# Weights of v in pairs, h in rows of 512 tokens, gates and gelus in DRAM by fours, gates stored from the sync engine

## The chip, the core and the metric

One core of a Trainium2 chip runs one transformer block (batch 1, 512 tokens, width 1024) from one launch. The metric is the device time of that launch in microseconds. TensorE's clock is granted by the chip at 1.2 or 2.4 GHz; a granted clock of 1.00 in the profile is 2.4 GHz.

## The reference

The block is adaLN, a mixer of three kinds of attention, and a feed-forward layer of the PEER kind. The change touches the last. For each token it scores 8 heads x 2 x 128 keys, takes the best 16 of 16384 experts for each head, and adds up their rows:

```
q = einsum(h, wq);  s = einsum(q, sub_keys)          # 2 x 128 keys per head
top, eidx = the 16 best of the 16384 pairs;  g = softmax(top)
a = gelu(einsum(u[eidx], h));  out = einsum(g * a, v[eidx])
x = x + g2 * out;  return rmsnorm(x, final_g)
```

All is float32. u and v have 16384 rows of 1024 numbers, 64 MB each.

## The kernel before

The 512 tokens are four tiles of 128. For the first tile (128 tokens x 128 chosen experts) GpSimd gathers one row of u and one of v per token and expert (L1203 to L1219), and VectorE does the product with h and the sum into y0 (L2121, L2098). For the other three tiles, 384 tokens, nothing is gathered: the 16384 experts are taken in 128 chunks of 128, and every expert is computed for every token. Three things are made for each chunk:

- a = u h: TensorE, 24 matmuls of 384 columns (`a_chunk`, L843 to L860). Each float32 operand is split into a high part in the fast format (float32r) and a low part, the rest, and three products are taken: u_hi h_hi, u_hi h_lo, u_lo h_hi. ScalarE copies u_raw to u_hi (`u_high`, L1428), VectorE or GpSimd makes u_lo = u_raw - u_hi (L2131, L2002; L1200 for the first 17 chunks), and ScalarE takes gelu of a into one of 8 slots of a_act (L1471).
- the gates: a matrix of 128 experts x 384 tokens that holds the softmax weight where a token has chosen an expert and 0 elsewhere. They are made before the loop, in 12 blocks of 32 tokens x all 16384 experts, and put in DRAM.
- v: TensorE, 18 matmuls of 512 columns (`v_chunk`, L897 to L909) that add w_hi v_hi, w_hi v_lo, w_lo v_hi to six banks of PSUM, where w is gate times gelu.

h_hi and h_lo are laid out [tile, k, 128 tokens] (L162), so the 384 tokens of one k are three pieces of 128 columns, 4 KB apart. `q_passes` (L804) reads the same two tensors for wq.

**Order of the work.** It is written out by hand for every engine, with semaphores. TensorE does the first u chunks while VectorE chooses the experts. Then come three parts, one for each tile (the gates' stage): in a part four blocks of gates (`tb`), each of eight groups. A group is small matmuls of hot rows into bank T (L885), made by VectorE (L2057, L2059) and copied by ScalarE into g_out (L1505, two buffers of 16 KB a partition, `g_out[tb % 2]`), and a quarter of a chunk of u beside them. Between the parts only chunks of u run (`BETWEEN`, L366: chunks 0 to 23, 32 to 35, 44 to 51, 60 to 63), while VectorE decodes the next tile's experts; the last of them is cut in two halves, around three transposes into bank G (L870).

At the end of a block ScalarE waits for its last copy and issues the store of 2 MB (L1511, L1512). The chunks' gelus of 0 to 55 are stored too (`spill`, L1483) and come back for the late stage (L1096).

```
gates = nc.dram_tensor("gates", [DT // GB, P, NCHUNK, GB], f32).ap()     # L296
spill = nc.dram_tensor("spill", [SPILL, P, DT], f32).ap()                # L297
BETWEEN = [range(0, 24), range(32, 36), range(44, 52), range(60, 64)]    # L366
return BETWEEN[tb // 4].stop + 2 * (tb % 4)                              # beside(tb), L376
```

So a block's run in DRAM is 16 KB a partition (128 experts' numbers x 32 tokens), and one load for four chunks (`load_g`, L1088) takes 12 runs of 512 B a partition.

**The sync engine's queue** (L1076 to L1132) issues the loads of u (each waits until the chunk two before it is split, s_ulo), of v (four buffers, waits for s_vlo), of gates and of the gelus. `load_g(0)` comes after the loads of u for chunks 64 and 65, and waits for all stores of gates (s_gst).

**The loop** over the chunks of v (`chunk_loop`, L314) has 128 turns. In turns 0 to 62 TensorE does a chunk of v and one of u (up to 1291 us of the profile), afterwards (the late stage) one of v alone. VectorE's `weigh` (L2069 to L2089) does for every chunk: the product w_f (L2076), its high part w_hi (L2085), its low part w_lo (L2087), 384 columns each; then v_lo (L2108), the first tile's products and sums, and u_lo (L2131). ScalarE's `parts` (L1524) does v_hi, the small gelus and weights of the first tile, u_hi and the gelu. The last four chunks have buffers of their own (`..._end`, L198 to L201).

Of the kernel before, what the change touches and what calls it, by code (L numbers as in the profile page):

```python
# [6 lines left out]
P = 128  # L7
D, S = 1024, 512
KD = D // P
# [9 lines left out]
GT = 1  # L19
# [78 lines left out]
def peer_block_kernel(nc, x, c_col, norm1_col, w_ada, b_ada, w_in, w_out, lam_vecs, subln_row, sinks_row,  # L98
# [4 lines left out]
    with ctx:  # L103
# [9 lines left out]
        def at(name, kib, shape, dt=f32):  # L113
# [34 lines left out]
        wo_hi = [at(f"wo_hi{k}", kib, [P, D], f32r) for k, kib in enumerate((24, 28, 44, 76))]  # L148
# [13 lines left out]
        h_hi = at("h_hi", 32, [P, NT, KD, P], f32r)  # L162
        h_lo = at("h_lo", 64, [P, NT, KD, P], f32r)
# [14 lines left out]
        y0 = at("y0", 32, [P, D])  # L178
        g_in = at("g_in", 56, [P, 2, DT // GB, 4, GB])
# [5 lines left out]
        u_lo = [at(f"u_lo{j}", kib, [P, D], f32r) for j, kib in enumerate((92, 84))]  # L185
# [5 lines left out]
        w_f = at("w_f", 128, [P, DT])  # L191
        w_hi = at("w_hi", 130, [P, 2, DT], f32r)
        w_lo = at("w_lo", 133, [P, 2, DT], f32r)
        rows = [at(f"row{j}", k, [P, D]) for j, k in enumerate((104, 108, 136, 168, 176, 184,
                                                                     140, 144, 148, 152, 156, 160))]
        junk = at("junk", 180, [P, D])
# [4 lines left out]
        w_lo_end = at("w_lo_end", 176, [P, TAIL, DT], f32r)  # L201
# [94 lines left out]
        gates = nc.dram_tensor("gates", [DT // GB, P, NCHUNK, GB], f32).ap()  # L296
        spill = nc.dram_tensor("spill", [SPILL, P, DT], f32).ap()  # L297
# [6 lines left out]
        def after(eng, s, n):  # L304

            if isinstance(n, int) and n < 1:
                return
            eng.wait_ge(s, n)

# [109 lines left out]
        def out_hi(k, half=None):  # L419

            if k == 4:
                return v_r[:, :, 192:448] if half is None else v_r[:, 2 * half:2 * half + 2, 192:448]
            t = wo_hi[k] if k < 4 else wo_hi_c[k - 5]
            return t[:, :] if half is None else t[:, half * 512:half * 512 + 512]

# [30 lines left out]
        def _(pe):  # L456
# [347 lines left out]
            def q_passes(e, tiles):  # L804

                ps = bank[f"S{e % 3}"][:, tiles.start * P:tiles.stop * P]
                pe.wait_ge(s_qhi, e + 1)
                pe.wait_ge(s_qlo, e + 1)
                for k in range(KD):
                    kk = slice(k * P, k * P + P)  # L810
                    pe.matmul(ps, wq_hi_of(e)[:, kk], h_hi[:, tiles, k, :], start=(k == 0), stop=False)
                    pe.matmul(ps, wq_hi_of(e)[:, kk], h_lo[:, tiles, k, :], start=False, stop=False)
                    mm = pe.matmul(ps, wq_lo[e % 2][:, kk], h_hi[:, tiles, k, :], start=False, stop=(k == KD - 1))
# [29 lines left out]
            def a_chunk(i, c, part=range(KD)):  # L843
# [10 lines left out]
                for k in part:  # L854
                    kk = slice(k * P, k * P + P)
                    pe.matmul(ps[:, 0:DT], u_hi[q][:, kk], h_hi[:, GT:NT, k, :], start=(k == 0), stop=False)  # L856
                    pe.matmul(ps[:, 0:DT], u_hi[q][:, kk], h_lo[:, GT:NT, k, :], start=False, stop=False)  # L857
                    mm = pe.matmul(ps[:, 0:DT], u_lo[q][:, kk], h_hi[:, GT:NT, k, :], start=False, stop=(k == KD - 1))  # L858
# [38 lines left out]
            def v_chunk(i, c):  # L897

                pe.wait_ge(s_w, i + 1)
                pe.wait_ge(s_vlo, i + 1)  # L900
                q = c % 2
                first = isinstance(i, int) and i == 0
                for t in range(NT - GT):
                    tt = slice(t * P, t * P + P)
                    for n, (w, v) in enumerate(((w_hi, v_hi), (w_hi, v_lo), (w_lo, v_hi))):
                        for half in range(2):
                            mm = pe.matmul(y_bank[t][half][:, :], w[:, q, tt], v[:, q, half * 512:half * 512 + 512],  # L907
# [3 lines left out]
            def last_v_chunks():  # L911
# [8 lines left out]
                def chunk_ready(m):  # L920
                    pe.wait_ge(s_w, m + 1)
# [68 lines left out]
        def _(sp):  # L990
# [1242 lines left out]
```

## Time and profile before

| | |
|---|---|
| three runs | 1567.2, 1567.73, 1568.44 us; median 1567.73 |
| the profiled execution: span from first to last instruction | 1565.4 us |
| its own whole time | not given by the profile |
| TensorE matmul / weight load | 1527.4 us (98%) / 1363.9 us (87%) |
| VectorE / ScalarE / GpSimd | 1337.7 us (85%) / 660.1 us (42%) / 487.5 us (31%) |
| mean granted clock of TensorE | 0.995 |
| DMA | 398.77 MB, mean 255 GB/s |
| store of a block of gates, issue to landing, median of 12 | 6.8 us |

"Busy" counts matmuls as they overlap, so it says that TensorE had work, not that it ran at its best. Register, branch and semaphore instructions are not counted. A row of the timeline has the start, the duration, engine, line, operation, and output<-inputs; in square brackets stands the idle time before it and what ended it. bank_S, bank_T, bank_O and bank_G are banks of PSUM; PEld is TensorE's weight load. The rows stand in a section further down.

### The profile page before, as it was taken

How to read it: one execution, taken by the hardware profiler on the slowest of the kernel's cores; microseconds unless marked ns; L12 is line 12 of the kernel's file. 1: busy time of each engine (PE TensorE's matmuls, PEld its weight loads, DVE VectorE, ACT ScalarE, POOL GpSimd, SP SyncE). 2: the span in 40 equal slices, each digit the busy share in tenths (PEclk: the TensorE clock that was granted, in tenths of full speed). 3: DMA queues.
4: the chain of work that ended last, by engine and by line, in shares of the span. 5: the costliest groups of instructions: out<-in, count | busy, mean ns of one | idle time of the engine just before them, and what ended most of it. 6: DMA issues, size and time to landing. Idle time of an engine off the chain costs nothing.

```text
span 1565.4 us, 24588 instructions
## 1 busy us (share of the span) xinstructions
PE 1527.4 (98%) x8275; PEld 1363.9 (87%) x8275; DVE 1337.7 (85%) x2877; ACT 660.1 (42%) x1143; POOL 487.5 (31%) x450
## 2 busy tenths in 40 slices
PE   4999999999999999999999999999999999999997
PEld 4887767888999999999999999999999998888886
DVE  5788666549999989899698898899999998999977
ACT  3444554233344757657433333343333332333232
POOL 1121300033450000020355455456566663233000
PEclk9999999999999999999999999999999999999999
DMA  9754410132355565676899999999999999999772
GB/s 366 270 174 148 148 68 0 55 95 82 118 169 180 194 230 199 229 248 251 298 393 330 350 340 343 346 337 371 372 378 372 368 345 355 376 350 352 241 244 104
DMA packets 160467, 398.77 MB, mean 255 GB/s; under 512 B 11753, under 2 KB 75369, under 8 KB 158705
## 3 DMA queue, kind: packets, MB, share of 16 engines
q1 hardware_dynamic: 112992, 227.06, 41.7%
q0 software_dynamic: 36864, 134.23, 23.2%
q10 hardware_dynamic: 10514, 36.30, 5.9%
q8 instruction: 47, 0.77, 0.2%
q14 instruction: 50, 0.41, 0.1%
HBM read 359.27 MB, written 38.27 MB: 254 GB/s over the span
## 4 chain that ended last, share of the span: by engine, by line
PE 83%; DVE 13%; DMA 1%; ACT 1%; issue 1%; ACTq 0%; DVEq 0%; SPq 0%
PE bank_S L907 16%; PE bank_T L907 11%; PE bank_O L858 6%; PE bank_O L856 6%; PE bank_O L857 6%; PE bank_T L885 5%; PE bank_G L907 5%; PE bank_S L856 3%; PE bank_S L857 3%; PE bank_S L858 3%; PE bank_O L643 2%; PE bank_S L610 2%; DVE mod_acc L1909 1%; DVE v_sb L1902 1%; DVE v_sb L1915 1%; DVE si L1921 1%
## 5 line engine op out<-in xcount | busy, mean ns | idle before, releaser
L1462 ACT ACTIVATE v_hi<-v_raw 128x1024 fp32r<-128x1024 f32 x124 | 131.7, 1062 | 333.9 <-PE bank_G L907 330.9
L1434 ACT ACTIVATE u_hi<-u_raw 128x1024 fp32r<-128x1024 f32 x128 | 135.9, 1061 | 243.0 <-PE bank_O L858 122.8
L1213 POOL COPY stage<-eidx 128x1 uint32<-128x1 uint32 (+1 forms) x128 | 75.7, 591 | 461.8 <-DVE eidx L2030 207.7
L1217 POOL DMA_INDIRECT row<-in_peer_u,stage x128 | 148.1, 1157 | 103.8 <-POOL stage L1213 103.8
L856 PE MATMUL bank_S<-h_hi,u_hi 128*128 128x384 f32 x512 | 179.7, 351 | 0.5 <-DVE u_lo L2002 0.5
L858 PE MATMUL bank_O<-h_hi,u_lo 128*128 128x384 f32 x512 | 171.9, 336 | 0.0
L856 PE MATMUL bank_O<-h_hi,u_hi 128*128 128x384 f32 x512 | 171.7, 335 | 0.0
L858 PE MATMUL bank_S<-h_hi,u_lo 128*128 128x384 f32 x512 | 171.5, 335 | 0.0
L857 PE MATMUL bank_O<-h_lo,u_hi 128*128 128x384 f32 x512 | 171.5, 335 | 0.0
L857 PE MATMUL bank_S<-h_lo,u_hi 128*128 128x384 f32 x512 | 171.4, 335 | 0.0
L2098 DVE SCALAR_TENSOR_TENSOR y<-row,wgt,y 128x1024 f32<-128x1024 f32 x128 | 165.9, 1296 | 0.0
L2108 DVE TENSOR_TENSOR v_lo<-v_raw,v_hi 128x1024 fp32r<-128x1024 f32 x124 | 152.0, 1226 | 12.1 <-ACT v_hi L1462 0.6
L2121 DVE SCALAR_TENSOR_TENSOR junk<-row,h 128x1024 f32<-128x1024 f32 x128 | 155.8, 1217 | 0.0
L1217 POOL DMA_INDIRECT row<-in_peer_v,stage x128 | 141.6, 1106 | 41.9 <-issue 30.3
L907 PE MATMUL bank_S<-v_hi,w_lo 128*128 128x512 f32 x372 | 125.4, 391 | 0.0
L907 PE MATMUL bank_S<-v_lo,w_hi 128*128 128x512 f32 x372 | 125.3, 391 | 0.0
L907 PE MATMUL bank_S<-v_hi,w_hi 128*128 128x512 f32 x372 | 125.2, 391 | 0.0
L1505 ACT ACTIVATE g_out<-bank_T 128x512 f32<-128x512 f32 x96 | 104.7, 1122 | 46.6 <-PE bank_T L885 38.2
L2057 DVE TENSOR_SCALAR hot_i<-iota_k,cols 128x128 f32<-128x128 f32 x384 | 106.6, 341 | 1.0 <-PE bank_T L885 0.2
L885 PE MATMUL bank_T<-hot_i,hot_j 128*128 128x128 f32 x768 | 101.8, 275 | 1.2 <-DVE hot_j L2059 1.2
L885 PEld LDWEIGHTS bank_T<-hot_i,hot_j 128*128 128x128 f32 x768 | 97.6, 191 | 3.6 <-issue 2.1
L856 PEld LDWEIGHTS bank_O<-h_hi,u_hi 128*128 128x128 f32 x512 | 96.1, 188 | 2.5
(370 smaller groups left out, 3647.8 us busy)
## 6 DMA issues: line engine op xcount, KB each, us to landing
u_raw<-in_u_t SPq DMA_DIRECT2D x128, 512.0 KB
v_raw<-in_peer_v SPq DMA_DIRECT2D x128, 512.0 KB
gates<-g_out ACTq DMA_DIRECT2D x12, 2048.0 KB, 6.8
g_in<-gates SPq DMA_DIRECT2D x32, 768.0 KB
ada_late<-in_w_ada SPq DMA_DIRECT2D x8, 2048.0 KB, 8.4
spill<-a_act ACTq DMA_DIRECT2D x56, 192.0 KB, 2.1
a_act<-spill SPq DMA_DIRECT2D x14, 768.0 KB, 10.6
w_raw<-in_w_in SPq DMA_DIRECT2D x20, 512.0 KB, 4.1
```

The source lines that it names most:

```text
L856: pe.matmul(ps[:, 0:DT], u_hi[q][:, kk], h_hi[:, GT:NT, k, :], start=(k == 0), stop=False)
L857: pe.matmul(ps[:, 0:DT], u_hi[q][:, kk], h_lo[:, GT:NT, k, :], start=False, stop=False)
L858: mm = pe.matmul(ps[:, 0:DT], u_lo[q][:, kk], h_hi[:, GT:NT, k, :], start=False, stop=(k == KD - 1))
L885: mm = pe.matmul(ps[:, tok * P:tok * P + P], hot_j[:, b % 2, tok, :], hot_i[:, b % 2, tok, :], start=True, stop=True)
L907: mm = pe.matmul(y_bank[t][half][:, :], w[:, q, tt], v[:, q, half * 512:half * 512 + 512], start=(first and n == 0), stop=False)
L1217: pool.indirect_dma_start(rows[slot][:, :], None, table[:, :], bass.IndirectOffsetOnAxis(stage[:, place:place + 1], 0))\
L1434: act.activation(u_hi[c % 2][:, :], u_raw[:, c % 2, :], ACT.Copy).then_inc(s_uhi, 1)
L1462: act.activation(v_hi_end[:, i % TAIL, :] if end else v_hi[:, c % 2, :], v_raw[c % 4][:, :], ACT.Copy)\
L2057: dve.tensor_scalar(hot_i[:, B % 2, tok, :], iota_k[:, :], cols[:, 0, n:n + 1], cols[:, 2, n:n + 1], ALU.is_equal, ALU.mult)
L2098: dve.scalar_tensor_tensor(out=y0[:, :], in0=rows[2 * place + 1][:, :], scalar=wgt[:, q], in1=y0[:, :], op0=ALU.mult, op1=ALU.add).then_in ...
L2108: dve.tensor_tensor(lo[:, q, :], v_raw[c % 4][:, :], hi[:, q, :].bitcast(f32), ALU.subtract)\
L2121: dve.scalar_tensor_tensor(out=junk[:, :], in0=rows[2 * place][:, :], scalar=1.0, in1=h2[:, 0, :], op0=ALU.mult, op1=ALU.mult, accum_out=d ...
```

## The change

- h_hi and h_lo are [k, 512 tokens], so the moving operand of `a_chunk` and `q_passes` is one run. The two tensors' first 128 columns of each k (the first tile's) are no longer needed after wq: u_lo of every second chunk lies in h_lo's, y0 in h_hi's, each in eight pieces of 128 (`by_k`). GpSimd's `split_u(1)` waits until the last q is done.
- The product is made for two chunks at once, in place in g_in, by VectorE; ScalarE copies its high part (`w_high`), VectorE subtracts (`w_low`). w_hi and w_lo have two buffers of two chunks. The product of a pair is made one chunk ahead, w_high is issued at the end of ScalarE's even chunks.
- gates is [partition, four of chunks, block, 4, 32], spill [four, partition, 4, 384]. A block's store now writes 32 runs of 512 B a partition, a load of gates reads one run of 6 KB a partition, and so does a load of gelus.
- The stores of gates go from ScalarE's to the sync engine's queue, after the load of u four chunks past `beside(tb)`.
- The product of the first tile (L2121) writes over the gathered row instead of into junk; rows, g_in, w_hi, w_lo and w_lo_end have other places in SBUF. The first tile's last squares go to rows[2].

```diff
-        h_hi = at("h_hi", 32, [P, NT, KD, P], f32r)
-        h_lo = at("h_lo", 64, [P, NT, KD, P], f32r)
+        h_hi = at("h_hi", 32, [P, KD, S], f32r)
+        h_lo = at("h_lo", 64, [P, KD, S], f32r)
-        y0 = at("y0", 32, [P, D])
-        g_in = at("g_in", 56, [P, 2, DT // GB, 4, GB])
+        y0 = at("y0", 32, [P, KD, S])[:, :, 0:P]
+        g_in = [at(f"g_in{j}", kib, [P, DT // GB, 4, GB]) for j, kib in enumerate((56, 182))]
-        u_lo = [at(f"u_lo{j}", kib, [P, D], f32r) for j, kib in enumerate((92, 84))]
+        u_lo = [at("u_lo0", 92, [P, KD, P], f32r)[:, :, :], h_lo[:, :, 0:P]]
-        gates = nc.dram_tensor("gates", [DT // GB, P, NCHUNK, GB], f32).ap()
-        spill = nc.dram_tensor("spill", [SPILL, P, DT], f32).ap()
+        gates = nc.dram_tensor("gates", [P, NCHUNK // 4, DT // GB, 4, GB], f32).ap()
+        spill = nc.dram_tensor("spill", [SPILL // 4, P, 4, DT], f32).ap()
...
-                    pe.matmul(ps[:, 0:DT], u_hi[q][:, kk], h_hi[:, GT:NT, k, :], start=(k == 0), stop=False)
+                    pe.matmul(ps[:, 0:DT], u_hi[q][:, kk], h_hi[:, k, GT * P:S], start=(k == 0), stop=False)
...
-                pe.wait_ge(s_w, i + 1)
+                pe.wait_ge(s_w, over(i, c, 2) + 1)
...
-                    after(sp, s_pw, 4 * (q - 1))
-                    sp.dma_start(g_in[:, parity, :, :, :].rearrange("p b i t -> p b (i t)"),
-                                 gates[:, :, bass.ds(chunk_of(4 * q, late), 4), :].rearrange("b p i t -> p b (i t)"))\
+                    after(sp, s_w, 2 * (q - 1))
+                    own = q - MAIN // 4 if late or (isinstance(q, int) and 4 * q >= MAIN) else q + SPILL // 4
+                    sp.dma_start(g_in[parity][:, :, :, :].rearrange("p b i t -> p (b i t)"),
+                                 gates[:, bass.ds(own, 1), :, :, :].rearrange("p o b i t -> p (o b i t)"))\
...
+            def store_gates(tb):
+
+                sp.wait_ge(s_gt, (tb + 1) * (GB // 4))
+                sp.dma_start(gates[:, :, tb, :, :].rearrange("p q i t -> p q (i t)"),
+                             g_out[tb % 2][:, :, :].rearrange("p (q i) t -> p q (i t)", i=4)).then_inc(s_gst[tb % 2], 16)
+
+            STORES = {beside(tb) + 4: tb for tb in range(BLOCKS)}
             for i in range(2, EARLY):
                 load_u(i, i)
+                if i in STORES:
+                    store_gates(STORES[i])
                 m = i - (EARLY - 5)
...
+                if i == 1:
+                    taken(pool, ("q", 2 * PH - 1))
                 pool.wait_ge(s_uhi, i + 1)
...
+            def w_high(i, c):
+
+                if not within(i):
+                    return
+                if at_end(i):
+                    act.wait_ge(s_acc, PH * TOPK)
+                else:
+                    after(act, s_yv, i - 2)
+                act.wait_ge(s_pw, over(i, c, 2) + 1)
+                act.activation(weight_pair(w_hi, w_hi_end, i, c), gate_pair(c), ACT.Copy).then_inc(s_whi, 1)
...
-                    act.wait_ge(s_gt, (tb + 1) * (GB // 4))
-                    act.dma_start(gates[tb].rearrange("p i t -> p (i t)"),
-                                  g_out[tb % 2][:, :, :].rearrange("p i t -> p (i t)")).then_inc(s_gst[tb % 2], 16)
...
+                if c % 2 == 0:
+                    w_high(m + 2, c + 2)
...
+                dve.tensor_tensor(gate_pair(c), by_block(a_act[:, slot:slot + 2, :]), gate_pair(c), ALU.mult)\
+                   .then_inc(s_pw, 1)
+
+            def w_low(i, c):
+
+                dve.wait_ge(s_whi, over(i, c, 2) + 1)
+                if not at_end(i):
+                    after(dve, s_yv, i - 2)
+                dve.tensor_tensor(weight_pair(w_lo, w_lo_end, i, c), gate_pair(c),
+                                  weight_pair(w_hi, w_hi_end, i, c).bitcast(f32), ALU.subtract).then_inc(s_w, 1)
...
             def chunk(i, c, late, numbers):
-                weigh(i, c, late)
+                if c % 2 == 0:
+                    w_low(i, c)
+                else:
+                    product(i + 1, c + 1)
```

## Rows read from the trace of the kernel before

**Rows 1.** Table of stretches: length, busy us and instructions of each engine, TensorE's clock, DMA share, GB/s.

```profile
500.00:600.00 100.00, 99.15 (x677) 97.53 (x676) 93.72 (x231) 62.80 (x70) 0.00 (x0) 1.00 0.56 200
...
768.00:1031.00 263.00, 263.00 (x1330) 239.22 (x1329) 236.65 (x310) 99.06 (x194) 141.60 (x148) 1.00 0.95 349
```

**Rows 2.** Timeline of TensorE, early stage: start us, us, engine, line, operation.

```profile
429.01 0.33 PE L856 MATMUL bank_S<-h_hi,u_hi 128*128 128x384 f32 x1
...
432.13 0.33 PE L856 MATMUL bank_S<-h_hi,u_hi 128*128 128x384 f32 x1
```

**Rows 3.** Chain of waits, loop and late stage: start us, us, what.

```profile
1100.32 1.62 PE bank_S L907 x7
1108.63 1.62 PE bank_S L907 x7
...
1454.62 1.59 PE bank_S L907 x7
1458.70 1.59 PE bank_S L907 x7
```

**Rows 4.** Timeline of TensorE after a group of small matmuls, gates' stage.

```profile
589.40 0.42 PE L856 MATMUL bank_S<-h_hi,u_hi 128*128 128x384 f32 x1
589.66 0.34 PE L857 MATMUL bank_S<-h_lo,u_hi 128*128 128x384 f32 x1
```

**Rows 5.** Groups by line and shape, whole span: count | busy us, mean ns | idle us before.

```profile
L2108 DVE TENSOR_TENSOR v_lo<-v_raw,v_hi 128x1024 fp32r<-128x1024 f32 x124 | 152.0, 1226 | 12.1 <-ACT v_hi L1462 0.6 <-DVE w_lo L2087 0.3
...
L1434 ACT ACTIVATE u_hi<-u_raw 128x1024 fp32r<-128x1024 f32 x128 | 135.9, 1061 | 243.0 <-PE bank_O L858 122.8 <-PE bank_S L858 79.3 <-DMA u_raw<-in_u_t 18.2
...
L2076 DVE TENSOR_TENSOR w_f<-a_act,g_in 128x384 f32<-128x384 f32 x128 | 70.4, 550 | 1.1 <-ACT a_act L1471 1.0
...
L2087 DVE TENSOR_TENSOR w_lo<-w_f,w_hi 128x384 fp32r<-128x384 f32 x124 | 69.4, 559 | 4.3
...
L2085 DVE CAST w_hi<-w_f 128x384 fp32r<-128x384 f32 x124 | 45.2, 365 | 47.5 <-PE bank_G L907 40.4 <-DVE w_f L2076 0.4
...
L1200 POOL TENSOR_TENSOR u_lo<-u_raw,u_hi 128x1024 fp32r<-128x1024 f32 x17 | 40.8, 2398 | 35.7 <-ACT u_hi L1434 35.7
...
L1471 ACT ACTIVATE a_act<-bank_O 128x384 f32<-128x384 f32 x64 | 30.3, 474 | 4.7 <-PE bank_O L858 4.7
```

**Rows 6.** DMA, 762 to 764 us (load of gates), then 652 to 656 us (store).

```profile
DMA packets 1224, 0.63 MB, mean 315 GB/s; under 512 B 8, under 2 KB 1222, under 8 KB 1224
...
DMA packets 108, 1.77 MB, mean 442 GB/s; under 512 B 0, under 2 KB 0, under 8 KB 0
```

**Rows 7.** Timeline of ScalarE, VectorE and TensorE at the end of the first part.

```profile
580.69 1.06 ACT L1434 ACTIVATE u_hi<-u_raw 128x1024 fp32r<-128x1024 f32 x1 [3.92 <-DMA u_raw<-in_u_t]
...
581.86 1.23 DVE L2002 TENSOR_TENSOR u_lo<-u_raw,u_hi 128x1024 fp32r<-128x1024 f32 x1 [1.75 <-ACT u_hi L1434]
...
588.52 1.13 PE L885 MATMUL bank_T<-hot_i,hot_j 128*128 128x128 f32 x8 [0.40 <-DVE hot_j L2059]
```

**Rows 8.** Timeline of VectorE and TensorE at the end of the second part.

```profile
661.49 1.22 DVE L2002 TENSOR_TENSOR u_lo<-u_raw,u_hi 128x1024 fp32r<-128x1024 f32 x1 [1.60 <-ACT u_hi L1434]
...
663.23 0.33 PE L856 MATMUL bank_S<-h_hi,u_hi 128*128 128x384 f32 x1
```

**Rows 9.** Timeline at the end of the third part and the start of the loop.

```profile
745.63 0.43 SPq L1085 DMA_DIRECT2D v_raw<-in_peer_v  x1
...
747.41 0.34 ACTq L1512 DMA_DIRECT2D gates<-g_out  x1
...
757.72 1.23 DVE L2002 TENSOR_TENSOR u_lo<-u_raw,u_hi 128x1024 fp32r<-128x1024 f32 x1 [3.95 <-ACT u_hi L1434]
...
759.58 0.33 PE L856 MATMUL bank_S<-h_hi,u_hi 128*128 128x384 f32 x1
...
765.45 0.57 DVE L2076 TENSOR_TENSOR w_f<-a_act,g_in 128x384 f32<-128x384 f32 x1 [1.02 <-ACT a_act L1471]
...
767.89 0.63 PE L907 MATMUL bank_S<-v_hi,w_hi 128*128 128x512 f32 x2
```

More of the change, by code:

```diff
@@ L308, in after, with half_columns, by_k, gate_pair @@
             eng.wait_ge(s, n)
+        def half_columns(h, i, half):
+            return h[:, 4 * half:4 * half + 4, i * P:i * P + P]
+        def by_k(row):
+            return row.rearrange("p (k c) -> p k c", k=KD)
+        def gate_pair(c):
+            return g_in[c // 4 % 2][:, :, c % 4:c % 4 + 2, :].rearrange("p b i t -> p i b t")
+        def by_block(pair):
+            return pair.rearrange("p i (b t) -> p i b t", t=GB)
+        def weight_pair(w, w_end, i, c):
+            if at_end(i):
+                q = i % TAIL
+                return by_block(w_end[:, q:q + 2, :])
+            return by_block(w[c // 2 % 2][:, :, :])
         def within(i, last=NCHUNK - 1):
@@ L422, in out_hi, with in_pieces @@
                 return v_r[:, :, 192:448] if half is None else v_r[:, 2 * half:2 * half + 2, 192:448]
+            if k in (2, 3):
+                last = (h_hi, h_lo)[k - 2][:, :, (NT - 1) * P:S]
+                return last if half is None else last[:, 4 * half:4 * half + 4, :]
             t = wo_hi[k] if k < 4 else wo_hi_c[k - 5]
             return t[:, :] if half is None else t[:, half * 512:half * 512 + 512]
+        def in_pieces(k, whole):
+            pieces = {2: KD, 3: KD, 4: NT}
+            return whole.rearrange("p (t c) -> p t c", t=pieces[k]) if k in pieces else whole
         def wq_hi_of(e):
@@ L804, in q_passes @@
             def q_passes(e, tiles):
+                columns = slice(tiles.start * P, tiles.stop * P)
                 ps = bank[f"S{e % 3}"][:, tiles.start * P:tiles.stop * P]
@@ L855, in a_chunk @@
                     kk = slice(k * P, k * P + P)
-                    pe.matmul(ps[:, 0:DT], u_hi[q][:, kk], h_hi[:, GT:NT, k, :], start=(k == 0), stop=False)
-                    pe.matmul(ps[:, 0:DT], u_hi[q][:, kk], h_lo[:, GT:NT, k, :], start=False, stop=False)
-                    mm = pe.matmul(ps[:, 0:DT], u_lo[q][:, kk], h_hi[:, GT:NT, k, :], start=False, stop=(k == KD - 1))
+                    pe.matmul(ps[:, 0:DT], u_hi[q][:, kk], h_hi[:, k, GT * P:S], start=(k == 0), stop=False)
+                    pe.matmul(ps[:, 0:DT], u_hi[q][:, kk], h_lo[:, k, GT * P:S], start=False, stop=False)
+                    mm = pe.matmul(ps[:, 0:DT], u_lo[q][:, k, :], h_hi[:, k, GT * P:S], start=False, stop=(k == KD - 1))
                 if part[-1] == KD - 1:
@@ L1798, in h_low @@
                 dve.wait_ge(s_hhi, 2 * i + half + 1)
-                part = slice(4 * half, 4 * half + 4)
-                dve.tensor_tensor(h_lo[:, i, part, :], ps[:, :].rearrange("p (a b) -> p a b", b=P),
-                                  h_hi[:, i, part, :].bitcast(f32), ALU.subtract)\
+                dve.tensor_tensor(half_columns(h_lo, i, half), ps[:, :].rearrange("p (a b) -> p a b", b=P),
+                                  half_columns(h_hi, i, half).bitcast(f32), ALU.subtract)\
                    .then_inc(freeing(("h2T", i, half)), 1)
@@ L2097, in row_sum @@
                 dve.wait_ge(s_got[2 * place + 1], 16 * (over(n, c, RING) + 1))
-                dve.scalar_tensor_tensor(out=y0[:, :], in0=rows[2 * place + 1][:, :], scalar=wgt[:, q], in1=y0[:, :],
+                dve.scalar_tensor_tensor(out=y0, in0=by_k(rows[2 * place + 1][:, :]), scalar=wgt[:, q], in1=y0,
                                          op0=ALU.mult, op1=ALU.add).then_inc(s_acc, 1)
@@ L2120, in chunk @@
                     dve.wait_ge(s_got[2 * place], 16 * (over(n, g, RING) + 1))
[L2121 removed]
+                    dve.scalar_tensor_tensor(out=rows[2 * place][:, :], in0=rows[2 * place][:, :], scalar=1.0,
+                                             in1=h2[:, 0, :],
                                              op0=ALU.mult, op1=ALU.mult, accum_out=dots[:, g % 4:g % 4 + 1])\
```

86 lines of the change are left out of this document (37 added, 49 removed).

## The prediction

> **What bounds the kernel now.** I read the table of stretches first. In 500 to 600 us TensorE's matmuls are busy 99.15 of 100 us, in 768 to 1031 all 263 of 263, at a granted clock of 1.00 (2.4 GHz); VectorE stands at 93.72 and 236.65 in the same stretches [rows 1]. So from the gates' stage to the end of the loop over the chunks of v the time is the number of TensorE's instructions times its step, and what another engine saves is worth nothing unless TensorE waits for it. Next the step itself. A busy share of 100% could hide slow matmuls, so I took starts from the chain and the timeline. In the early stage 18 matmuls of 384 columns take 432.13 - 429.01 = 3.12 us, 173.3 ns each [rows 2]; in the late stage a chunk of v (18 matmuls of 512 columns) takes 1458.70 - 1454.62 = 4.08 us, 226.7 ns each [rows 3]. At 2.4 GHz both are the columns plus 32 cycles. The first has the moving operand h_hi in three pieces of 128 columns, the second a plain row: same surcharge. In the loop a chunk of v with one of u takes 1108.63 - 1100.32 = 8.31 us [rows 3] against 4.08 + 24 x 0.1733 = 8.24.
>
> TensorE has few waits after that. Where it nearly waits is what decides here: at the ends of the three parts of the gates' stage, where a chunk of u must be loaded while a block of gates is being stored.
>
> **h in rows of 512 tokens.** It removes the pieces of the moving operand: 24 matmuls in each of 128 chunks read 384 columns in one run. As the pieces cost nothing in the steps above, I cost this at nothing. The bound on the gain is what the steps leave over: 63 chunks x 0.07 us = 4.4 us in the loop, and in the gates' stage the step after the small matmuls, 589.66 - 589.40 = 0.26 us instead of 0.173, 96 times: 8.3 us [rows 4]. The low part of every second chunk of u and y0 now lie in eight pieces inside h_lo and h_hi. VectorE pays nothing for pieces: its product with the gates reads twelve pieces of 32 in 550 ns, its plain subtraction of the same size takes 559 [rows 5]. GpSimd's subtraction is known plain alone, 2398 ns [rows 5]. A chunk of u must be split while TensorE does one, 24 x 0.1733 = 4.16 us: 1.06 on ScalarE, 2.40 on GpSimd, some 0.3 of hops, which leaves 0.4.
>
> **Weights in pairs.** For two chunks VectorE now pays 2 x (550 + 365 + 559) = 2948 ns [rows 5]. Afterwards it does two instructions of 768 columns. Between 384 columns (559) and 1024 (v_lo, 1226) a column costs 1.04 ns [rows 5], so 768 take 0.95 us each, 1.90 in all: 0.52 us less per chunk. ScalarE gets one of 768: between 474 (384 columns) and 1061 (1024) 0.83 us per pair [rows 5]. None of this is on the path: TensorE does not wait for VectorE in the loop [rows 1]. ScalarE's new instruction waits for the product that VectorE makes at the start of the next chunk; behind it on ScalarE stands v_hi of the same later chunk. Even so 0.83 + 1.06 us are over before VectorE, busy at least 0.95 + 1.22 + 1.22 us in that chunk, asks for v_hi. Gelu's slots are free earlier than before. Taken at 0.
>
> **Gates and gelus by fours.** A block of gates is 2 MB. It was written in runs of 16 KB, and is now written in runs of 512 B; the loads in the loop change the other way, from 512 B to 6 KB. The number of short runs is the same (12 blocks x 4096 against 32 loads x 1536, 49152 each), but they move from the loop, where nobody waits for DMA, to the gates' stage. What short runs cost I take from loads, since the trace has no such store: 1224 packets, 1222 of them under 2 KB, in 2 us, so 612 a microsecond [rows 6]. A block has 128 x 32 = 4096 of them: 6.7 us. The old store moved 108 packets of 16 KB in 4 us [rows 6], 27 a microsecond, so 128 take 4.7 us. A store occupies the 16 engines 2.0 us longer.
>
> The Trainium skill's "DMA: Bandwidth & Descriptors", Specifications, gives 512 B as the least transfer that still runs at line rate. The trace does not agree: in [rows 6] the short runs moved 315 GB/s and the long ones 442. By the rule the store would stay at 4.7 us.
>
> **Stores on the sync engine's queue.** ScalarE is freed of the issue and of a wait for its own last copy, which is not on the path, since TensorE has no wait for ScalarE there. On the sync engine a store stands behind the load of u four chunks ahead of its block, and waits for the block's last copy; inside a part the next load of u is asked for half a block later, so nothing is held up. At a part's end it is: the next load of u is asked for as soon as the chunk two before is split, some 3 us after the store is issued, into the same queue, and every byte of it comes after the store's. Already now such a load lands only when the store is through: ScalarE waited 3.92 us for it [rows 7]. So the load lands later by what the store lasts longer, 2.0 us.
>
> First end: from 580.69 on the path runs without a gap from the landing over u_hi, u_lo (581.86), VectorE's decoding and the hot rows to TensorE's 0.40 us wait at 588.52 [rows 7]. Nothing covers it: +2.0 us. Second end: u_lo ends 661.49 + 1.22 = 662.71 and TensorE needs it at 663.23 [rows 8]: slack 0.5, so +1.5 us. Third end: here the load of v, issued at 745.63, stood before the store of 747.41 [rows 9]; now it is issued after it and delays u by another 512 KB, 1.2 us at 442 GB/s. The landing moves by 3.2 us; u_lo ended at 757.72 + 1.23 = 758.95, needed at 759.58 [rows 9]: slack 0.6, +2.6 us.
>
> Start of the loop: the first load of gates is issued after the load of u that waits for this u_lo, so also 3.2 us later; in 6 KB runs it takes 0.7 us less (768 KB at 442 instead of 315 GB/s). The first product moves from 765.45 to 767.95. Then 0.95 (product of a pair) + 0.83 (ScalarE) + 0.95, with hops of 0.05: ready at 770.8. TensorE, which took up v at 767.89 [rows 9], arrives at 767.89 + 2.6 = 770.5: +0.3 us.
>
> **Sum.** 2.0 + 1.5 + 2.6 + 0.3 = +6.4 us on the profiled execution (span 1565.4). Its own whole time is not given; the three runs lie 1.8 to 3.0 above the span, the median 2.3. So 1565.4 + 2.3 + 6.4 = 1574.1. What is late next: nothing; each stall delays TensorE, and all others catch up behind it.
>
> The Trainium skill's "DMA: Bandwidth & Descriptors", Queues, rings and completion order, says that each DMA engine goes round between the queues it has work for, and takes one queue in order. By that the load of u has so far shared the engines with the store, and would lose most of a store's time by the move, about 5 us, three times, which would give about 1582. The landing at 580.69, after 3.92 us of waiting, speaks against the first half of that, and so it has no more than 0.02, within the 0.05 of (c) below.
>
> **The rivals.**
> (a) Short writes run as fast as long ones, or they finish under cover. For: spills in runs of 1.5 KB hold nobody up. Against: the 315 GB/s of [rows 6]. Then the ends cost 0, 0 and 1.2 - 0.6 = 0.6 us and the loop's start about 0.4 more: 1568.7.
> (b) Faster: the surcharges in the steps (0.07 us a chunk of the loop, 0.09 us after each group of small matmuls) belong to the three pieces. For: they stand where h is read. Against: chunks of v in the loop, which read no h, are slow too (1.62 us for 7 against 1.59 [rows 3]), and the early stage reads the same pieces at 173.3 ns [rows 2]. It decides once 6.4 us are given back, that is if more than half of 4.4 + 8.3 = 12.7 us goes: 1574.1 - 12.7 = 1561.4.
> (c) Short writes are dearer than short reads. Bound: twice, 13.4 us a store. The ends then cost 8.7 + 8.2 + 9.3 and the start 0.3: 1594.2.
> (d) GpSimd is slow on the eight pieces. Past its 0.4 us of slack every second chunk of seventeen stalls; at 3.3 instead of 2.4 us that is 8 x 0.5 = 4 us more: 1578.1.
> (e) That the change does not do what it says: the relief of VectorE and of DMA in the loop is real and is simply not felt. That is part of the forecast.
>
> **How the numbers follow.** The forecast has 0.55, with a range of its own of 1571 to 1580 (0.5 us more or less at each of three ends for the store, and up to 1.5 us a place if writes cost a third more). (a) has 0.18, (b) 0.12, (c) 0.05, (d) 0.06, and 0.04 is left for a small gain that I do not see. About 0.2%, 3.1 us, is what a measurement of this kernel can tell from no change. Slower: 0.55 + 0.05 + 0.06 less what of the forecast falls under 3.1 us, 0.64. Within: 0.20. Faster: 0.16. The range 1564 to 1581 leaves out (c) and most of (b), under 2 in 10.
>
> **What would show it.** In the changed profile: stores of gates from the sync engine landing in 8.5 to 9 us instead of 6.8; three waits of TensorE for u_lo or hot rows at about 585 to 590, 663 and 760, of 1.5 to 2.6 us; VectorE's busy time down by 0.52 us a chunk, ScalarE's up by 0.42, TensorE's step of 173.3 and 226.7 ns unchanged. The forecast is wrong if the loop's 8.31 us falls towards 8.24 and the step after the small matmuls to 0.17 (b), if the loads of u at the three ends land as before (a), or if TensorE waits in the stage from 400 to 470 us (d).

## The result, and the profile after

The changed kernel takes 1581.33 us (median of 4 runs, 1578.97 to 1583.78), the kernel before 1568.09 us beside it (4 runs, 1567.2 to 1569.34): ratio 1.0085, interval 1.0072 to 1.0097. Slower by 13.2 us; forecast were 6.4. The profiled execution has a span of 1579.6 us against 1565.4, 14.2 more.

The page of the changed kernel, span and busy time:

```profile
span 1579.6 us, 24179 instructions
...
PE 1531.1 (97%) x8275; PEld 1367.1 (87%) x8275; DVE 1269.4 (80%) x2621; ACT 705.9 (45%) x1207; POOL 546.4 (35%) x450
```

The page of the kernel before has 1527.4 us for PE and 1337.7 for VectorE. So VectorE was relieved of 68 us, 0.53 a chunk, and that bought nothing. TensorE, with the same 8275 matmuls, is *busy* 3.7 us longer, which no wait can explain. Keep that number.

Groups by line and shape of the changed kernel, the new work on the weights (columns as in [rows 5]):

```profile
L2130 DVE TENSOR_TENSOR g_in<-a_act,g_in 128x768 f32<-128x768 f32 x64 | 60.9, 951 | 1.8 <-DMA g_in<-gates 1.8
L2138 DVE TENSOR_TENSOR w_lo<-g_in,w_hi 128x768 fp32r<-128x768 f32 x62 | 59.1, 953 | 2.8 <-ACT w_hi L1515 2.7
L1515 ACT ACTIVATE w_hi<-g_in 128x768 fp32r<-128x768 f32 x62 | 51.7, 834 | 0.2 <-DVE g_in L2130 0.2
```

The estimates were 0.95, 0.95 and 0.83 us. In the chain of waits, a chunk of v with one of u in the loop and one of v alone in the late stage answer to [rows 3]:

```profile
1106.12 1.62 PE bank_S L936 x7
1114.43 1.62 PE bank_S L936 x7
...
1460.57 1.59 PE bank_S L936 x7
1464.65 1.58 PE bank_S L936 x7
```

8.31 and 4.08 us, to the hundredth what they were: the pieces of h had cost nothing. The timeline of TensorE after a group of small matmuls answers to [rows 4], 0.26 us again:

```profile
592.95 0.42 PE L885 MATMUL bank_S<-h_hi,u_hi 128*128 128x384 f32 x1
593.21 0.34 PE L886 MATMUL bank_S<-h_lo,u_hi 128*128 128x384 f32 x1
```

Now the ends of the parts. What TensorE waited for, in three stretches (510 to 600, 600 to 700, 700 to 800 us; total, times, longest):

```profile
PE bank_S L885 <- DVE h_lo L2052: 2.6, 1, 2.6
PE bank_T L914 <- DVE hot_j L2109: 0.5, 1, 0.5
...
PE bank_S L885 <- DVE h_lo L2052: 2.7, 1, 2.7
...
PE bank_S L885 <- ACT u_hi L1475: 3.7, 1, 3.7
```

Before there were two waits of 0.4 us for hot rows in these stretches and nothing else. (h_lo is here the name of the place in which the low part of each odd chunk of u now lies.) The first end in the timelines of the sync engine, ScalarE and TensorE, which answers to [rows 7]:

```profile
571.82 0.55 SPq L1138 DMA_DIRECT2D gates<-g_out  x1
574.10 24.29 SPq L1109 DMA_DIRECT2D u_raw<-in_u_t  x5
...
584.24 1.06 ACT L1475 ACTIVATE u_hi<-u_raw 128x1024 fp32r<-128x1024 f32 x1 [6.95 <-DMA u_raw<-in_u_t]
...
586.77 0.41 PE L885 MATMUL bank_S<-h_hi,u_hi 128*128 128x384 f32 x1 [2.63 <-DVE h_lo L2052]
```

The load of u is asked for at 574.10 and landed at 584.15, 10.05 us; before it took 6.42. A store of gates lands 10.1 us after its issue (median of 12), before 6.8; the prediction's own sign was 8.5 to 9. The third end in the sync engine's timeline, which answers to [rows 9]:

```profile
755.17 0.55 SPq L1138 DMA_DIRECT2D gates<-g_out  x1
755.76 5.43 SPq L1115 DMA_DIRECT2D v_raw<-in_peer_v  x1
761.23 1.85 SPq L1109 DMA_DIRECT2D u_raw<-in_u_t  x2
```

The load of v behind the store took 5.43 us just to be *issued*. The chain of waits at the second end, which answers to [rows 8], shows the landing and then something that the prediction does not have:

```profile
656.74 10.09 DMA u_raw<-in_u_t
666.91 1.07 ACT u_hi L1475
668.07 1.24 DVE h_lo L2052
...
670.74 0.32 PE bank_S L885
671.06 0.32 PE bank_S L886
```

From 1.3 us after the end of the wait (at 669.44) each matmul of 384 columns takes 0.32 us instead of 0.173. The table of stretches (columns as in [rows 1]) gives the reason, in its third column from the right, the granted clock; before, all of these read 1.00:

```profile
670.00:675.00 5.00, 5.00 (x22) 5.00 (x21) 4.61 (x6) 0.24 (x1) 0.00 (x0) 0.66 0.76 227
...
765.00:770.00 5.00, 2.50 (x15) 2.18 (x13) 0.15 (x1) 1.24 (x2) 0.00 (x0) 0.95 0.62 249
770.00:775.00 5.00, 3.78 (x12) 3.81 (x13) 4.43 (x4) 2.46 (x4) 0.00 (x0) 0.50 0.55 199
775.00:780.00 5.00, 5.00 (x27) 5.00 (x26) 0.97 (x1) 1.96 (x3) 2.28 (x4) 0.86 0.65 227
```

The granted clock fell to 0.50, 1.2 GHz, for 3.4 us in all after the second wait and for 6.8 us at the third. There it fell at 769.54, while TensorE still stood (its wait ended at 771.22), so 5.2 us of the 6.8 met matmuls. That is where the 3.7 us more of "busy" come from.

**Where the 14.2 us are.** I followed one instruction after another along TensorE in both traces: late by 0.9 at the first group of small matmuls (509.42 against 508.52), +2.64 at the first end, +2.67 at the second, +1.68 in the half clock behind it, +3.75 at the third, +2.47 in the half clock behind that; from the start of the loop to the end no more (+14.1 at both). Waits 9.1, clock 4.15, start 0.9. (The figures at the first two ends are read at the next group of small matmuls.) The 0.9 is no part of what costs at the ends: TensorE is late by it already at 46 us, long before the first store of gates. I count it as the spread of single executions: in thirteen of the fourteen profiles taken here, of kernels that up to there do nearly the same, that group began between 508.35 and 509.80 (e1: 510.48), and in the one without either move of the gates (e3) at 509.34.

### The profile page after: what moved, and what is told of

It is laid out like the page before. It is cut to its first block, busy times and chain, and to the rows that moved or that the text cites. A ratio compares the mean times of both kernels' runs of the same rounds, so it can differ in the third digit from the quotient of the medians.

```text
span 1579.6 us, 24179 instructions
## 1 busy us (share of the span) xinstructions
PE 1531.1 (97%) x8275; PEld 1367.1 (87%) x8275; DVE 1269.4 (80%) x2621; ACT 705.9 (45%) x1207; POOL 546.4 (35%) x450
## 4 chain that ended last, share of the span: by engine, by line
PE 82%; DVE 13%; DMA 3%; ACT 1%; issue 1%; DVEq 0%; SPq 0%; ACTq 0%
PE bank_S L936 16%; PE bank_T L936 11%; PE bank_O L887 6%; PE bank_O L885 6%; PE bank_O L886 6%; PE bank_T L914 5%; PE bank_G L936 5%; PE bank_S L885 3%; PE bank_S L886 3%; PE bank_S L887 3%; DMA u_raw<-in_u_t 2%; PE bank_O L671 2%; PE bank_S L638 2%; DVE mod_acc L1959 1%; DVE v_sb L1965 1%; DVE v_sb L1952 1%
## 5 line engine op out<-in xcount | busy, mean ns | idle before, releaser
L1255 POOL COPY stage<-eidx 128x1 uint32<-128x1 uint32 (+1 forms) x128 | 98.8, 772 | 417.5 <-DVE eidx L2080 214.7
L1259 POOL DMA_INDIRECT row<-in_peer_u,stage x128 | 160.8, 1256 | 104.0 <-POOL stage L1255 102.9
L1259 POOL DMA_INDIRECT row<-in_peer_v,stage x128 | 164.9, 1288 | 41.9 <-issue 41.6
L2174 DVE SCALAR_TENSOR_TENSOR row<-row,h 128x1024 f32<-128x1024 f32 x128 | 156.9, 1226 | 0.0
L885 PEld LDWEIGHTS bank_S<-h_hi,u_hi 128*128 128x128 f32 x512 | 97.9, 191 | 11.1 <-issue 7.1
L886 PEld LDWEIGHTS bank_O<-h_lo,u_hi 128*128 128x128 f32 x512 | 96.2, 188 | 2.5
## 6 DMA issues: line engine op xcount, KB each, us to landing
gates<-g_out SPq DMA_DIRECT2D x12, 2048.0 KB, 10.1
```

Source lines behind the costliest of these rows:

```text
L885: pe.matmul(ps[:, 0:DT], u_hi[q][:, kk], h_hi[:, k, GT * P:S], start=(k == 0), stop=False)
L886: pe.matmul(ps[:, 0:DT], u_hi[q][:, kk], h_lo[:, k, GT * P:S], start=False, stop=False)
L1259: pool.indirect_dma_start(rows[slot][:, :], None, table[:, :], bass.IndirectOffsetOnAxis(stage[:, place:place + 1], 0))\
L2174: dve.scalar_tensor_tensor(out=rows[2 * place][:, :], in0=rows[2 * place][:, :], scalar=1.0, in1=h2[:, 0, :], op0=ALU.mult, op1=ALU.mult, ...
```

## The experiments

Theory: the loss is the load of u standing behind a store of short runs in one queue, three times, plus the slow clock. Rivals: the queue alone, the short runs alone, or the weights in pairs and h.

**Two by two.** Three kernels undo one or both of the moves of the gates, a fourth puts both into the kernel before.

e1, back to ScalarE's queue, runs of 512 B kept:

```
-                if i in STORES:
-                    store_gates(STORES[i])
...
+                    act.wait_ge(s_gt, (tb + 1) * (GB // 4))
+                    act.dma_start(gates[:, :, tb, :, :].rearrange("p q i t -> p q (i t)"),
+                                  g_out[tb % 2][:, :, :].rearrange("p (q i) t -> p q (i t)", i=4))\
```

> The changed kernel, with the stores of gates issued by ScalarE again, in runs of 512 B as now. Theory A (the load of u lands only when the store of the other queue is through, so the queue does not matter and the length of the store does): the loads of u at the three ends land about as late as now, TensorE waits 2 to 3 us at each; the load of v stands ahead of the store again, which saves 1.2 us and perhaps the slow clock at the third end: 1576 to 1580. Theory B (the engines take turns between two queues, one packet of each: 8 packets of 4 KB of u per engine alternate with 8 packets of the store; these were 16 KB before, so that both ended together at 6.4 us, and are 512 B here, so that u is through after some 2 us): u lands within 3 us of its issue, no wait at the three ends, not even the 0.4 us of before: 1567 to 1568.

e2, back to runs of 16 KB, sync engine kept; e3 has both edits:

```
-        gates = nc.dram_tensor("gates", [P, NCHUNK // 4, DT // GB, 4, GB], f32).ap()
+        gates = nc.dram_tensor("gates", [DT // GB, P, NCHUNK, GB], f32).ap()
...
-                sp.dma_start(gates[:, :, tb, :, :].rearrange("p q i t -> p q (i t)"),
+                sp.dma_start(gates[tb].rearrange("p i t -> p (i t)"),
```

> The changed kernel, with the gates in DRAM laid out as before: stores in runs of 16 KB, loads in runs of 512 B; the stores stay on the sync engine's queue. Both theories: behind the whole store in one queue, u lands after 2 MB and 512 KB at 442 GB/s, 5.9 us, as before at the first two ends; at the third the load of v comes between, 1.2 us, less 0.6 of slack. 1568 to 1570. If the queue alone costs the time, whatever the runs (rival), it stays above 1578.

> The changed kernel, with both undone: stores by ScalarE in runs of 16 KB, loads of gates of 512 B. What is left is the weights in pairs, h in rows of 512 tokens and the gelus by fours. If these are free, as predicted: 1568.1, within 1. If they carry part of the 13 us (rival: hidden gain or loss), it differs from before by over 2 us.

e5, the same lines of the diff put into the kernel before (store_gates on the sync engine, gates by fours):

> The kernel before, with only the layout of the gates by fours and the stores on the sync engine's queue. If the whole loss lies in these two, 1581, within 1.5, with TensorE's three waits of 2.6, 2.7 and 3.7 us and a half clock after the second and third. If the loss needs the pairs as well (their longer start of the loop behind the late load of gates), 2 us or more less.

Measured beside the kernel before (1567.76), 5 executions of e1, 11 each of e2 and e3:

| stores | by ScalarE | by the sync engine |
|---|---|---|
| runs of 16 KB | e3 1568.80 (1.0007, 0.9998 to 1.0016) | e2 1568.83 (1.0008, 0.9999 to 1.0017) |
| runs of 512 B | e1 1618.72 (1.0324, 1.0309 to 1.0338) | changed kernel 1581.33 |

e5: 1581.88 (1.0088, 1.0075 to 1.0102), with waits of 2.5, 2.4 and 3.8 us; a half clock came at the third alone, not at the second as expected. So there is no loss without the short runs; with long ones the queue alone costs nothing; and the rest of the change costs about 1 us, which the intervals do not tell from none (-0.3 to 2.5 us by e3). How much of the loss with short runs belongs to what stands behind them in the queue, e6 shows below. That rest shows as one wait of e3 between 700 and 800 us, at the start of the loop (e2 has 0.8 there):

```profile
PE bank_S L936 <- DVE w_lo L2132: 0.7, 1, 0.7
```

It is the term that the prediction put at 0.3; in the changed kernel it hides behind the third end's stall.

e1 fell out of both theories, by 39 us and more. Its ScalarE, timeline at the first end:

```profile
571.22 0.54 ACTq L1555 DMA_DIRECT2D gates<-g_out  x1
571.86 1.06 ACT L1466 ACTIVATE u_hi<-u_raw 128x1024 fp32r<-128x1024 f32 x1 [0.67 <-ACT g_out L1548]
572.83 0.47 ACT L1514 ACTIVATE a_act<-bank_S 128x384 f32<-128x384 f32 x1
573.33 3.99 ACTq L1526 DMA_DIRECT2D spill<-a_act  x1
577.71 1.88 ACT L1548 ACTIVATE g_out<-bank_T 128x512 f32<-128x512 f32 x2 [4.41 <-issue]
```

The spill of a gelu, the next DMA in the same queue, holds its engine for 3.99 us at its issue (0.33 for a spill with no such store ahead). Behind it stands the next copy out of PSUM, and TensorE waits for that (500 to 800 us):

```profile
PE bank_T L914 <- ACT g_out L1548: 31.1, 8, 5.0
```

That wait comes eight times, and eight stretches of half clock go with it (34 us in all). It is the same hold as the 5.43 us of v in the changed kernel; the sync engine has nothing else to do, ScalarE has.

**Nothing behind the store.** e6 is e1 with the spills of chunks 24 to 55 issued by GpSimd, idle at that time:

```
+            for i in range(BETWEEN[0].stop, SPILL):
+                pool.wait_ge(s_gelu, i + 1)
+                pool.dma_start(spill[i // 4, :, i % 4, :], a_act[:, i % AHEAD, :]).then_inc(s_asp[i % 2], 16)
```

> As e1 (stores of 512 B runs issued by ScalarE), but the gelus of chunks 24 to 55 are spilled by GpSimd, so that nothing stands behind a store in its queue. Theory A (e1 lost 50 us because ScalarE itself was held 4 us at the issue of the spill behind each store): ScalarE is never held, TensorE's waits for g_out go, and since the loads of u are in a queue of their own beside 512 B packets, the three waits at the ends are gone as well, the half clocks too; what is left is 0.7 us for w_lo at the start of the loop: 1568 to 1569. Theory B (e1's loss came from ScalarE's queue working through the short writes, whoever stands behind): stays above 1600.

1570.96 (1.0019, 1.0009 to 1.0028), 48 us under e1: the hold was e1's loss. It is also 10.4 us under the changed kernel, with the same short runs, v ahead of the last store again, and no half clock. But it is 2 us more than expected: TensorE waits 1.0 us at the first, at the second end and for w_lo, the last because the load of gates waits for a store that lands 13.8 us after its issue. The store goes through one queue (q10) and the load of u through another (q1), where nothing holds its issue. The sync engine's timeline, a line of the chain of waits, and DMA of e6 from 574 to 578 us:

```profile
573.95 0.33 SPq L1110 DMA_DIRECT2D u_raw<-in_u_t  x1
...
573.95 7.58 DMA u_raw<-in_u_t
```

```profile
DMA packets 2206, 1.13 MB, mean 282 GB/s; under 512 B 0, under 2 KB 2206, under 8 KB 2206
...
q10 hardware_dynamic: 2206, 1.13, 102.2%
```

Not one packet of u in 4 us; its first comes at 578.7, and it lands 7.6 us after its issue. The Trainium skill's "DMA: Bandwidth & Descriptors", Queues, rings and completion order, says that a DMA engine goes round between the queues that it has work for. For the first 4.7 us the trace shows no sign of that; from 578.7 to 581.7, when the store's last packet starts, packets of both queues go side by side. It doesn't show when the load's descriptors reached the DMA engines, so whether the engines passed them over or did not have them yet stays open. So the prediction was right not to count on an even share. But a queue of its own is most of the way round the store: the load landed 10.7 us after the issue of the store instead of 12.3, and the kernel loses 2.8 us instead of 13.2.

**Order at the ends.**

```
-            STORES = {beside(tb) + 4: tb for tb in range(BLOCKS)}
+            STORES = {beside(tb) + 4 + (tb in (3, 7)): tb for tb in range(BLOCKS)}
...
                     load_v(m, m, False)
+                if i in STORES:
+                    store_gates(STORES[i])
```

> The changed kernel, runs of 512 B on the sync engine's queue, but at the first two ends of a part the next load of u is issued ahead of the store, and at the third the load of v(3). Theory A (what costs is that the load of u stands behind the store): the loads of the first two ends land some 3 us after their issue, the waits of 2.6 and 2.7 us and the half clock behind the second go, 7.0 us; the load of u after it is not needed for another 10 us. At the third end the load of v no longer comes between, 1.2 us, and the wait falls from 3.7 to about 2.5. In all 1581.3 - 8.2 = 1573.1, and 3 less if the clock stays up at the third end. Theory B (4096 short writes are dear wherever they stand): the wait only moves to the next load of u, and it stays at 1579 or more.

e7 moves only the last store behind v(3), as e4 does, and leaves the other two ends alone.

> The changed kernel with one thing moved: the load of v(3) ahead of the last store. If v between store and u is worth its bytes alone: the third wait falls from 3.7 to 2.5 us, 1.2 us. If the half clock after it goes with the shorter wait, another 2.5: 1577.6 to 1580.1. If the hold of v's issue (5.4 us) is what sets u's landing, the wait falls by more than 1.2. Nothing changed at the other two ends.

e4: 1579.48 (1.0069, 1.0056 to 1.0083). Theory B holds for the total: the wait moved on. Its TensorE in the three stretches:

```profile
PE bank_T L914 <- DVE hot_j L2109: 3.5, 1, 3.5
...
PE bank_S L885 <- DVE u_lo L2052: 3.3, 1, 3.3
...
PE bank_S L885 <- DVE h_lo L2052: 1.5, 1, 1.5
```

The load of u after the store is held 3.54 us at its issue and is late in its turn; I had called it not needed for another 10 us. e7: 1579.07 (1.0067, 1.0053 to 1.0080). Its third wait is 2.9 us instead of 3.7, 0.8 less; but in e4, with the same edit at that end, it is 1.5, 2.2 less, and e7's first wait, where nothing was changed, is 3.2 instead of 2.6. So what v between store and u is worth stays open, from 0.8 to 2.2 us around the 1.2 of its bytes. The executions of both kernels spread over some 6 us, so the total says little more.

**Size of a run.** e8 has the gates by eights of chunks, 2048 runs of 1 KB a store.

```
-        gates = nc.dram_tensor("gates", [P, NCHUNK // 4, DT // GB, 4, GB], f32).ap()
+        gates = nc.dram_tensor("gates", [P, NCHUNK // 8, DT // GB, 8, GB], f32).ap()
```

> The changed kernel with the gates in DRAM by eights of chunks: stores of 2048 runs of 1 KB on the sync engine's queue, loads of gates in runs of 512 B again. Theory A (each short packet costs a fixed time, 29 ns for 512 B, and 1 KB moves at the 442 GB/s of the long ones, 37 ns): a store lasts 4.7 us as before, the waits at the ends are 0, 0 and 0.4 us as in the run with 16 KB runs on this queue: 1569. Theory B (what costs is any store of thousands of descriptors in one queue, by its number): half of the loss at the ends, with waits of about 1 us: 1572 to 1575.

1574.40 (1.0041, 1.0028 to 1.0055): theory B, half the loss, with waits of 1.7, 1.2, 1.4 and 0.6 us (the last for w_lo) and no slow clock in these stages. DMA from 573 to 577 us of e8:

```profile
DMA packets 1339, 1.38 MB, mean 346 GB/s; under 512 B 0, under 2 KB 1339, under 8 KB 1339
```

DMA from 574 to 578 us of e1:

```profile
DMA packets 2264, 1.16 MB, mean 290 GB/s; under 512 B 0, under 2 KB 2264, under 8 KB 2264
```

566 packets of 512 B a microsecond, or 335 of 1 KB. Theory A's 442 GB/s at 1 KB is refuted: 290, 346 and 442 GB/s for 512 B, 1 KB and 16 KB. The line rate from 512 B up that the Trainium skill's "DMA: Bandwidth & Descriptors", Specifications, states is not what these stores show, nor what the loads showed before. The length of a run, the number of descriptors and the steps between runs in DRAM changed together here; apart they were not tried.

**Is the slow clock a cost of its own?** e9 and e11 give TensorE 12, 12 and 18 matmuls to do at the three ends. In e9 they write to the bank of the chunk, in e11 to one that is free:

```
+                    if early and i in (35, 47, 63):
+                        pe.wait_ge(s_gt, {35: 32, 47: 64, 63: 96}[i] - 1)
+                        for _ in range(18 if i == 63 else 12):
+                            pe.matmul(bank["T0"][:, 0:DT], h_hi[:, 0, P:2 * P], h_hi[:, 0, GT * P:S], start=True, stop=True)
                     after(pe, s_gelu, i - 1)
```

> The changed kernel; TensorE fills its three waits with matmuls whose results are overwritten by the chunk that follows (12, 12 and 18 matmuls of 384 columns, 2.1, 2.1 and 3.1 us, ahead of its wait for the chunk of u). No load, store or other engine is touched. Theory A (the granted clock falls because TensorE stood still for 2.7 us and more, and that cost 4.15 us in the profiled execution beside the waits themselves): waits of about 0.5 us remain at each end, no half clock follows, and the time is 1581.3 - 4.2 = 1577, within 1. Theory B (the half clocks have another cause, or cost nothing of their own): 1581 as before, within 1, or more, if the filling delays the chunk.

> As e9, but the matmuls that fill (12, 12 and 18 of 384 columns) write to a bank of gates that is free there, so that they wait for nothing and begin where TensorE's wait began; in e9 they had to wait for a gelu first, 1.4 to 2.0 us, and then took up what they were to cover. Theory A (the half clock comes from TensorE standing still, and costs time of its own): waits of about 0.5 us are left at each end, no half clock follows, and the time is 3 to 4 us under the changed kernel run beside it. Theory B (half clocks come anyway, or their cost is hidden): within 1 us of it.

> The changed kernel once more, beside e11 on the same chip. 1581.3, within 1.5. Theory A of e11: its executions spread over 5 us since the half clocks that follow the waits are none, one or two stretches of 3.4 us in each place; in this profile too each wait of 2.7 us or more is followed by one and none of 2.6 or less.

e9 decides nothing: 1581.61 (1.0084, 1.0071 to 1.0098), where theory A had 1577, with one half clock of 3.4 us left. The matmuls had to wait 1.4, 1.6 and 2.0 us for a gelu before they could begin, and with their own 2.1 to 3.1 us covered more than the old waits. e11: 1576.43 (1.0052, 1.0038 to 1.0066), 4.0 us under e12, 1580.42 (1.0079, 1.0065 to 1.0093). All five of its executions lie within 0.6 us, those of e12 within 2.5. What is left of the waits in e11 at the first and the second end:

```profile
PE bank_S L889 <- DVE h_lo L2056: 0.5, 1, 0.5
...
PE bank_S L889 <- DVE h_lo L2056: 0.6, 1, 0.6
```

Its table of stretches, two of them:

```profile
660.00:680.00 20.00, 19.43 (x112) 19.14 (x111) 13.50 (x17) 5.75 (x8) 0.00 (x0) 1.00 0.70 220
765.00:785.00 20.00, 20.00 (x109) 18.78 (x108) 14.42 (x17) 11.15 (x18) 7.47 (x9) 1.00 0.74 280
```

Clock 1.00 throughout, while the load of u at the first end lands 10.04 us after its issue, as late as in the changed kernel. So the half clocks came from TensorE standing still. What they cost beside the waits is 4.0 us at most: at the first two ends fill and rest together last as long as e12's waits (2.6 us), but at the third TensorE is taken up for 3.2 us only, where e12 waited 3.9, since the load of u landed sooner after its store. That leaves about 3.3 us for the clock. e12's other expectation missed: its wait of 2.64 us at the second end was followed by a half clock too.

**A version without the loss?** e10 is e2 with the loop's first load of gates ahead of two loads of u.

```
+            for parity in range(2):
+                sp.wait_ge(s_gst[parity], 16 * (BLOCKS // 2))
+            load_g(0, 0, False)
             load_u(EARLY, 0)
             load_u(NEXT, 1)
```

> The run with 16 KB runs on the sync engine's queue (1568.8), with the first load of gates of the loop issued ahead of the loads of u of chunks 64 and 65. Theory A (what is left over the kernel before is TensorE's wait of 0.8 us for the first low part of the weights, since product, high and low part of a pair are a longer chain than those of one chunk): the load is issued some 3 us earlier, the wait goes: 1568.0, the same as before. Theory B (the chain waits for ScalarE or VectorE, not for the load): 1568.8 again; and if the load of u behind the gates is late in its turn, 1570 or more.

1569.66 (1.0010, 1.0001 to 1.0019): theory B. The wait of 0.8 us for w_lo stayed, and ahead of it stand two of 0.7 us for u, where e2 has one of 0.4. No version here beats the kernel before.

## Why the prediction was right and wrong

Right: the sign, the places, and that a load of u waits for a store of short runs. TensorE bounds; the steps of 173.3 and 226.7 ns stand; pairs, h in rows and GpSimd's eight pieces cost nothing where it was said. Rival (d), GpSimd slow on the pieces, is out, since TensorE has no wait from 340 to 475 us; (b), a gain, since the steps stand. Short writes are neither free (a) nor twice as dear as reads (c): 290 GB/s against 315. The loss is at the three ends. Not right was the size, 13.2 us instead of 6.4: one term was too small and one was missing. Step by step:

- "So the load lands later by what the store lasts longer, 2.0 us." This is the step that failed among the waits. From the issue of the store to ScalarE's start on the landed u it was 9.36, 9.23 and 9.21 us at the three ends before, and is 12.42, 12.45 and 13.59: 3.1, 3.2 and 4.4 us later, where the prediction had 2.0, 2.0 and 3.2. The DMA view of the kernel before at the first end, 572 to 578.5 us, spills included:

```profile
DMA packets 274, 2.31 MB, mean 356 GB/s; under 512 B 31, under 2 KB 135, under 8 KB 145
```

  The same of the changed kernel, 573 to 581.3 us:

```profile
DMA packets 4303, 2.37 MB, mean 285 GB/s; under 512 B 33, under 2 KB 4302, under 8 KB 4303
```

  From first to last packet the store lasted 6.2 us before and 8.2 after: both 1.5 longer than I had (4.7 and 6.7), the difference 2.0 as predicted. What is missing lies around it, by the packets' times in the two traces: the short store's first packet comes 1.2 us after its issue instead of 0.9 (+0.3), and the first packet of u comes 0.7 us after the store's last, where before it came at once (+0.7). 2.0 + 0.3 + 0.7 = 3.0. The 10.05 us from issue to landing instead of 6.42 say 0.6 more, but only since u is now asked for 2.28 us after the store instead of 2.86; that is so at the first two ends in every profile with the store on the sync engine ahead of u, whatever its runs, and asking sooner moves no landing that the store decides. The pause does not always come, e7 has none at its first end; what makes it was not tried.
- Waits at the ends: forecast 2.0, 1.5 and 2.6, measured 2.64, 2.67 and 3.75, 9.1 instead of 6.1. Order and slack were judged rightly: 3.1, 3.2 and 4.4 us less the slacks of 0, 0.5 and 0.6 are 3.1, 2.7 and 3.8. v between store and u was put at 1.2; e4 and e7 have 2.2 and 0.8.
- Start of the loop: forecast 0.3, measured 0 in the changed kernel and 0.7 to 0.8 in e2 and e3, where nothing stalls ahead of it.
- Missing altogether: "What is late next: nothing; each stall delays TensorE, and all others catch up behind it." This is the other step that failed, a term put at nothing. TensorE itself ran slower behind its waits: half clock, 4.15 us in the profiled execution, 3.3 to 4.0 by e11. With the 3.0 of the waits and the 0.9 at the start this is the difference, less 0.3.

The prediction gave 0.02 to 1582, by even turns between the queues, and 1581.3 was measured. The number is a coincidence: by that account u would lose its share of the engines by the move into the store's queue alone, but in e2, which makes that move with long runs, it lands 9.6 us after the store's issue instead of 9.3, and the time is 1568.83.

Theory B of e8 and e4, a price for each descriptor that is paid wherever the store stands, is what I should have weighed against "behind the store". It is not the whole of it either: in e6 all 4096 descriptors are still there and 10.4 us of the loss are gone.

## What to carry to other kernels

Cut a store into runs as long as its reader allows, and count the descriptors, not the bytes: 4096 of 512 B took 8.2 us on the engines where 128 of 16 KB took 6.2, and what is issued next on that queue may hold its engine for 4 to 5 us. Put such a store on a queue in which nothing urgent follows (e6 lost 2.8 us where the changed kernel lost 13.2), and look at what must land next, whichever queue it is in. Before moving short runs from one stage to another, ask which of the two has no slack: a stall of TensorE of some 3 us costs its own length and may cost some two thirds of it again in clock (1.68 on 2.67 us, 2.47 on 3.75, nothing on 2.64).

## What the runs showed of the hardware

- **An engine is held at the issue of a DMA behind one with thousands of descriptors.** Instead of 0.33 to 0.43 us: 3.99 (ScalarE, e1), 4.36 and 5.43 (sync engine, changed kernel), 3.54 (e4). Behind 2048 descriptors, 1.23 and 2.04 (e8). Counting packets, when a hold of 3.5 us or more ended, 610 to 1640 of the store's 4096 were still to start, in most cases 1270 to 1640; in e8's two 1290 and 1570 of 2048. An issue in the other queue is not held: in e6 the load of u takes 0.33. What limits it was not tried. Behind 128 descriptors of 16 KB a spill was issued in 0.88 us once and in 0.33 otherwise.
- **The clock after waits.** Waits of TensorE at the ends, of all profiles taken here but e1's and e9's, and the length of the half clock that began in their last 2 us or right behind: 1.0 to 1.7 us (e4, e6, e8), none; 2.4 to 2.7 (changed kernel, e5, e7, e12), none four times, 3.4 us twice and 6.8 once; 2.9 to 3.9 (the same and e4), 3.4 us three times and 6.8 four times. In e9 a wait of 2.0 us, with the filling matmuls behind it, was followed by 3.4 us too. So no sharp length comes out: a wait of 2.6 us was followed by a half clock in one place and not in another. That fits the executions of the changed kernel, which spread over 5 us, and those of e11, which do not.
- **Short writes have no fixed rate.** In e4, where the same store begins 3 us later, 680 packets a microsecond went out from 578 to 581 us (27 ns each) instead of e1's 566 (29 ns). Both stores were nearly alone on the engines in these stretches. Why is open.
